# Down projection of two column groups by seven block products instead of plain tiles, in a two-layer hybrid kernel on one core

## What is computed

```python
def swiglu(x, w_gate, w_up, w_down):
    return (jax.nn.silu(x @ w_gate) * (x @ w_up)) @ w_down
...
for l in range(DEPTH):
    x = x + 0.5 * swiglu(rms_norm(x, ffn1_norm[l]), ffn1_w_gate[l], ffn1_w_up[l], ffn1_w_down[l])
    x = x + hybrid_mixer(...)
    x = x + 0.5 * swiglu(rms_norm(x, ffn2_norm[l]), ffn2_w_gate[l], ffn2_w_up[l], ffn2_w_down[l])
```

## Time and profile before

| | |
|---|---|
| median of 3 runs | 2651.4 us (2651.0 to 2652.24) |
| the profiled execution: own time, span | 2651.94 us, 2650.2 us |
| mean granted TensorE clock | 0.999 |
| TensorE matmul busy | 2616.0 us, 99% of the span, 15716 instructions |
| VectorE, ScalarE, GpSimd busy | 1464.2, 1262.9, 1169.5 us (55, 48, 44%) |
| DMA | 240 MB, mean 91 GB/s |

### The profile page before, as it was taken

How to read it: one execution, slowest core, us unless ns; L and a number is a source line. 1 busy time by engine, 2 the same in 40 slices (tenths; PEclk the granted TensorE clock), 3 DMA queues, 4 the chain that set the end, 5 groups by cost and what they waited for, 6 DMA issues and landing times. The chain is left out here.

```text
span 2650.2 us, 41444 instructions
## 1 busy us (share of the span) xinstructions
PE 2616.0 (99%) x15716; PEld 2216.3 (84%) x15716; DVE 1464.2 (55%) x2231; ACT 1262.9 (48%) x2323; POOL 1169.5 (44%) x684
## 2 busy tenths in 40 slices
PE   7999999999999999999999999999999999999999
PEld 6999988766777788898988989887667778898998
DVE  7453574666556368263683535745665653773543
ACT  6453543655534336363464635345555344363543
POOL 4565644211322346565565655432122324465554
PEclk9999999999999999999999999999999999999999
DMA  4322223310111232232223232333012112232322
GB/s 148 112 96 98 103 103 105 110 49 30 71 60 60 84 111 101 96 112 96 96 96 108 100 112 84 107 108 107 33 41 72 61 60 91 104 105 96 112 96 96
DMA packets 38550, 240.46 MB, mean 91 GB/s; under 512 B 4321, under 2 KB 5601, under 8 KB 16353
## 3 DMA queue, kind: packets, MB, share of 16 engines
q1 hardware_dynamic: 36416, 233.85, 25.7%
q10 hardware_dynamic: 1952, 4.12, 0.4%
HBM read 234.81 MB, written 2.10 MB: 89 GB/s over the span
## 5 line engine op out<-in xcount | busy, mean ns | idle before, releaser
L351 POOL TENSOR_TENSOR wlo<-raw,whi 128x1024 fp32r<-128x1024 f32 (+1 forms) x310 | 687.1, 2217 | 1233.9 <-ACT whi L426 803.1
L1633 PE MATMUL bank<-hhi,whi 128*128 128x512 f32 x816 | 339.3, 416 | 15.5 <-DVE hlo L925 10.5
L1739 PE MATMUL bank<-th,slot_u 128*128 128x256 f32 x1152 | 326.3, 283 | 2.1 <-ACT tmp L549 2.1
L426 ACT ACTIVATE whi<-raw 128x1024 fp32r<-128x1024 f32 (+1 forms) x198 | 192.6, 974 | 283.8 <-PE bank L1635 158.1
L1740 PE MATMUL bank<-tl,slot_u 128*128 128x256 f32 x1152 | 326.0, 283 | 0.0
L1635 PE MATMUL bank<-hhi,wlo 128*128 128x512 f32 x816 | 321.0, 393 | 0.0
L1634 PE MATMUL bank<-hlo,whi 128*128 128x512 f32 x816 | 320.2, 392 | 0.0
L1633 PE MATMUL bank<-ff,whi 128*128 128x512 f32 x704 | 274.0, 389 | 0.0
L1634 PE MATMUL bank<-ff,whi 128*128 128x512 f32 x704 | 274.0, 389 | 0.0
L1635 PE MATMUL bank<-ff,wlo 128*128 128x512 f32 x704 | 273.9, 389 | 0.0
L416 ACT ACTIVATE whi<-raw 128x1024 fp32r<-128x1024 f32 (+1 forms) x96 | 96.7, 1008 | 370.4 <-PE bank L1635 370.4
(11 more groups left out here) (348 smaller groups left out, 6266.9 us busy)
## 6 DMA issues: line engine op xcount, KB each, us to landing
raw<-cb SPq DMA_DIRECT2D x48, 768.0 KB, 4.1
raw<-gu0a SPq DMA_DIRECT2D x16, 1024.0 KB, 5.0
raw<-gu0b SPq DMA_DIRECT2D x16, 1024.0 KB, 4.9
raw<-pM SPq DMA_DIRECT2D x16, 1024.0 KB, 4.9
raw<-cq SPq DMA_DIRECT2D x16, 1024.0 KB, 4.9
raw<-gu1a SPq DMA_DIRECT2D x16, 1024.0 KB, 4.8
raw<-gu1b SPq DMA_DIRECT2D x16, 1024.0 KB, 4.9
raw<-gu0c SPq DMA_DIRECT2D x12, 1024.0 KB, 4.9
```

The source lines that it names most:

```text
L351: pool.tensor_tensor(wlo[:, s, 0:w], raw[:, j, lo:lo + w], whi[:, s, 0:w].bitcast(f32), ALU.subtract).then_inc(sem["lo_done"], 1)
L426: A(whi[:, s, 0:(wa, wb)[s]], raw[:, u % 2, s * wa:s * wa + (wa, wb)[s]], ACT.Copy).then_inc(sem["hi_done"], 1)
L1633: mm(outp, wh, mhi, start=start and k == 0, stop=False)
L1739: mm(outp, wh, parts[k][0], start=start and k == 0, stop=False, skip_group_check=True)
```

## The change

The down projection of groups a and b is made by seven block products as well; group c stays plain. For this the hidden tiles of a group take the part of the data: the tile in the first half of the group (c < `KH` = 4) and the one four later are the rows of the 2 x 2 blocks, and token halves are the columns. A down unit makes two output tiles from 8 hidden tiles in 84 matmuls of 256 tokens. The sums of quarters that `th` holds for x have now to be made for the hidden tiles themselves, and for every group again: T3 = B22 - B12, and T2, T1, T4 from it, with highs and lows. They are made tile by tile, as each tile of the second half of a group comes out (`tile_parts`, `sum_highs`, `sum_lows`, and `tile_lows` on POOL). The plain tile of the first half is kept in fp32 (`uf`) beside its high and low. The first down unit after a gate-up unit ("turn") has another order of the products, since the sums of the last tile are still being made: A12, s4, A11, s3, s2, A22, s1, with s4 in a bank half of its own. Weight rows of the down projection are rotated by four tiles on the host.

```diff
-ORDER = ["A11", "A12", "s2", "s3", "s1", "A22", "s4"]
-SPLIT_AT = {0: 1, 1: 2, 4: 3, 3: 4, 2: 5, 5: 6, 6: 7}
...
+BLOCKS = {"reg": ["A11", "A12", "s2", "s3", "s1", "A22", "s4"], "turn": ["A12", "s4", "A11", "s3", "s2", "A22", "s1"]}
+BLOCKS["head"] = BLOCKS["reg"]
+HIGHS = {"head": (0, 1, 5, 4, 3, 2, 6), "reg": (0, 1, 4, 3, 2, 5, 6), "turn": (0, 1, 2, 3, 4, 5, 6)}
...
ScalarE
+                def tile_high(f, U):
...
+                    act.wait_ge(sem["st_p"], me.at("st_p", U.n + 1))
...
+                    elif U.c < KH:
+                        A(k2h[U.p][U.c], r[:], ACT.Copy).then_inc(sem["uhi_ready"], 1)
+                        A(uf[U.c], r[:], ACT.Copy).then_inc(sem["uf_ready"], 1)
+                    else:
+                        A(k1h[U.c - KH], r[:, 0:ST], ACT.Copy).then_inc(sem["uhi_ready"], 1)
+
+                def sum_highs(U):
...
+                    act.wait_ge(sem["u_sum"], me.at("u_sum", 4 * U.q + 1))
+                    A(thu[:, k, T3], tfu[:, k, T3], ACT.Copy).then_inc(sem["u_hi"], 1)
+                    act.wait_ge(sem["u_sum"], me.at("u_sum", 4 * U.q + 4))
+                    A(thu[:, k, T2], r[:, 0:ST], ACT.Copy).then_inc(sem["u_hi"], 1)
+                    A(thu[:, k, T1], r[:, ST:S], ACT.Copy).then_inc(sem["u_hi"], 1)
+                    A(thu[:, k, T4], tfu[:, k, T4], ACT.Copy).then_inc(sem["u_hi"], 1)
...
+                        if tile_before:
+                            late_silu(V)
+                        if U.kind == "turn":
+                            tile_high(f, V)
+                            sum_highs(V)
+                            block_high(6, U)
+                            act.sem_inc(sem["hi_done"], 2)
+                            block_copy(N)
+                            block_high(0, N)
+                            block_high(1, N)
+                            block_snap(p1s[j], bx[j], U, "A11")
+                            block_snap(p7s[j], bw[j], U, "s3")
+                            block_snap(u2s[j], bx[j], U, "s2")
...
VectorE
+                def tile_parts(U):
...
+                        dve.tensor_tensor(k1l[k], r[:, 0:ST], k1h[k].bitcast(f32), ALU.subtract).then_inc(sem["ulo_ready"], 1)
+                        dve.tensor_tensor(tfu[:, k, T3], tfu[:, k, T2], r[:, ST:S], ALU.subtract).then_inc(sem["u_sum"], 1)
...
+                        dve.scalar_tensor_tensor(r[:, 0:ST], tfu[:, k, T3], -1.0, r[:, 0:ST], ALU.mult, ALU.subtract).then_inc(sem["u_sum"], 1)
+                        dve.wait_ge(sem["u_sum"], me.at("u_sum", 4 * U.q + 2))
+                        dve.scalar_tensor_tensor(r[:, ST:S], r[:, 0:ST], -1.0, tfu[:, k, T2], ALU.mult, ALU.subtract).then_inc(sem["u_sum"], 1)
+                        dve.scalar_tensor_tensor(tfu[:, k, T4], r[:, 0:ST], -1.0, tfu[:, k, T4], ALU.mult, ALU.subtract).then_inc(sem["u_sum"], 1)
...
+                def sum_lows(U):
...
+                    dve.wait_ge(sem["u_hi"], me.at("u_hi", 4 * U.q + 3))
+                    dve.tensor_tensor(tlu[:, k, T2], r[:, 0:ST], thu[:, k, T2].bitcast(f32), ALU.subtract).then_inc(sem["u_low"], 1)
+                    dve.tensor_tensor(tlu[:, k, T1], r[:, ST:S], thu[:, k, T1].bitcast(f32), ALU.subtract).then_inc(sem["st_free"], 1)
...
+                        if U.kind == "turn":
+                            tile_parts(V)
+                            sum_lows(V)
+                            block_low(6, U)
+                            first_out(f, U)
+                            block_sums(N)
...
TensorE, the turn
+                        pe.wait_ge(sem["st_free"], me.at("st_free", n - 1))
...
+                        product(0)
...
+                        pe.wait_ge(sem["st_low"], me.at("st_low", 2 * n + 1))
+                        pe.wait_ge(sem["st_snap"], me.at("st_snap", 3 * n + 1))
+                        pe.wait_ge(sem["u_low"], me.at("u_low", V.q + 1))
+                        product(4)
```

More of the change, by code:

```diff
@@ L84, in widths, with block_units, split_at @@
     return WIDTHS.get(name, WIDTHS.get(name[:2], (KD * P, KD * P)))
[L87 to L95, removed]
+def block_units(f):
+    out, g, q = [], (KF - PLAIN) * f, 2 * KH * f
+    for p, (part, _, n) in enumerate(PASSES):
+        for c in range(0 if p else PLAIN, n):
+            u = FIRST[f"gu{f}{part}"] + c
+            out.append(Unit(u, NST * f + len(out), len(out), p, c, False, "reg" if out else "head", g, q))
+            g, q = g + 1, q + (p < 2 and c >= KH)
+        for c in range(KH if p < 2 else 0):
+            u = FIRST[f"dn{f}{part}"] + c
+            out.append(Unit(u, NST * f + len(out), len(out), p, c, True, "reg" if c else "turn", g, q))
+    return out
+def split_at(i, U):
+    return 7 * U.n + HIGHS[U.kind].index(i) + 1
 def build(nc, t, out):
@@ new lines, in _, with block_low @@
+                        unit(1, 0)
+                        unit(1, 1)
+                        units = block_units(f)
+                        def block_low(U, i):
+                            name = BLOCKS[U.kind][i]
+                            at = {"A11": 0, "A12": BLOCK, "A22": 3 * BLOCK}
+                            src = raw[:, U.u % 2, at[name]:at[name] + BLOCK] if name in at else s3[:] if name == "s3" else s4[:]
+                            pool.wait_ge(sem["st_hi"], me.at("st_hi", split_at(i, U)))
+                            return pool.tensor_tensor(bl[i], src, bh[i].bitcast(f32), ALU.subtract)
@@ L907, in _ @@
                 norm(2)
-                for p in range(len(PASSES)):
-                    ffn_pass(1, p)
+                ffn_blocks(1)
         @block.vector
@@ new lines, in ffn_blocks @@
+                def ffn_blocks(f):
+                    units = block_units(f)
+                    for U in units:
+                        V = units[U.i - 1] if U.i else None
+                        N = units[U.i + 1] if U.i + 1 < len(units) else None
+                        if V is None:
+                            plain_product(f, PLAIN - 1)
+                        elif V.down:
+                            down_close(f, V)
+                        else:
+                            block_product(V)
+                        if U.kind == "turn":
+                            tile_parts(V)
[3 more added lines that the diff above has]
+                            block_sums(N)
+                            block_low(4, N)
+                            third_out(f, U)
+                            block_low(2, N)
+                            fourth_out(U)
+                            continue
+                        first_out(f, U)
+                        if V is None:
+                            plain_low(f, PLAIN_ORDER[2])
+                            token_low(f, 3)
+                            plain_low(f, PLAIN_ORDER[3])
+                        elif not V.down:
+                            tile_parts(V)
+                        if V is not None and N:
+                            block_sums(N)
+                        fourth_out(U)
+                        if V is None:
+                            block_sums(N)
+                        if N and N.kind == "reg":
+                            block_low(4, N)
+                        third_out(f, U)
+                        if N:
+                            block_low(2 if N.kind == "reg" else 4, N)
+                        if V is not None and not V.down and V.p < 2 and V.c >= KH:
+                            sum_lows(V)
+                        if N is None:
+                            block_product(U)
+                            tile_parts(U)
+                    dve.wait_ge(sem["st_p"], me.at("st_p", NST * (f + 1)))
+                    dve.wait_ge(sem["st_free"], me.at("st_free", NST * (f + 1)))
```

492 lines of the change are left out of this document (282 added, 210 removed).

## The result

The changed kernel takes **2670.99 us** (median, 2669.49 to 2672.1) where the kernel before takes 2651.82 (2651.0 to 2652.3) on the same chip: a ratio of 1.0074, 95% interval 1.0062 to 1.0086. It is **slower by 19.2 us**, where I had forecast 4.6 less. The profiled execution has 2670.44 us and a span of 2668.6.

A forecast was written before the change was run, and what follows sets the result against it. TensorE's matmul time was taken as the bound, at 99% busy. Against the profiled execution's 2651.94 us, -25.8 + 19.6 + 1.2 + 0.4 = -4.6 gave 2647.3, forecast as 2647 us, range 2640 to 2655.

The forecast's parts named there:

- in one chain, from the end of the last gate-up unit (10.24) on: First down unit: dependent steps from late_silu to A11's snapshot at 18.08, starting product 4 at 18.29 instead of 15.84.
- The turn: First down unit after gate-up: product 4 waits for A11's late snapshot, 2.45 us each, 8 x 2.45 = 19.6 us.
- is not added, since the later chain covers it: Product 0 of the first down unit: its 0.8 us wait for VectorE's lows was left out of the sum.
- The clock: Rival, 3%: TensorE's clock falls at the turns, 2.4 us each, 19 us in all, giving 2666 us.
- the turn's waits are shorter: Argument against a clock fall: matmuls behind a 2.01 us wait ran at full speed, and waits in first down units are shorter.
- The matmuls' saving: Down sections of groups a and b: 40.32 us against 43.55, 3.23 us a section, 25.8 us saved in all.
- Product 6: Gate-up units behind a second-half tile: its bank's release comes up to 0.06 us late, in 20 units, 1.2 us.
- that rival: Rival, 11%: DVE's small instructions delay product 6's bank; at 0.5 us a unit 2656 us, with the turn's excess 2658.
- The first unit: First block unit: token_low(3) on DVE ends late for product 5; TensorE waits 0.1 us each, 0.4 in all.
- cheap turn: Rival, 12%: ACT's snapshot is not last to arrive, only product 0's 0.8 us remains in first down units; 2634 us.
- The rival of closer matmuls: Rival, 2%: matmuls of 256 run closer than 0.12 us (109 ns), some 12 us beyond the forecast, 2635 us.
- the third sign: Sign that the forecast is wrong: matmuls behind a turn take longer than 0.28 us.

The follow-up runs named there:

- the kernel with both moves: Changed kernel with ScalarE's s4 copy behind snapshot 7 in the last gate-up unit and the A11 snapshot earlier in the turn: 2640.12 us, ratio 0.9958 to before.
- the last experiment: The kernel with both moves, plus VectorE's low sums ahead of its combination and GpSimd's T3 low part one place earlier: 2632.66 us, ratio 0.9929 to before.
- two moves worth nothing each: On the kernel with both moves: VectorE's low sums earlier, 2641.37 us; GpSimd's T3 low part earlier, 2640.63 us; together 2632.66 us.
- the kernel before with seven copies: Kernel before plus seven idle ScalarE copies ahead of snapshot 7 in the last gate-up unit of groups a and b: 2681.29 us.
- the kernel with GpSimd's move alone: The kernel with both moves plus GpSimd's T3 low part one place earlier, VectorE's low sums left in place: 2640.63 us.

## Why the prediction was wrong

The four matmul, turn, product-6 and first-unit terms came to -4.6; measured was +19.2. The 24 us between them:

- **Missing altogether, 8 x 2.1 = 16.8 us: the last gate-up unit.** "in one chain, from the end of the last gate-up unit (10.24) on" was the step that failed. Product 5 of that unit waits 2.02 us by the distance of starts, 2.1 with the matmul behind it, and the sum had nothing for it. I took for granted that this unit runs like any other and began to count at its end. But its engines prepare the next unit, and the next unit is the turn, with another order of blocks: the copy that is free in a regular unit waits there for VectorE's last sum. The new order of blocks was in the diff, and my own count had the fourth sum start at 7.41 into such a unit and so end at 8.10, while product 5 wants its bank at 7.20. I used that count for product 6 alone. Moving that one copy recovered 17.1 us (13.6 by waits, 4.0 by the clock).
- **The turn, 3.07 instead of 2.45, 8 x 0.62 = 5.0 us.** The mechanism was right: product 0 waited on VectorE's lows and product 4 on the snapshot, and putting the snapshot earlier recovered 13.9 us, 1.62 in each group without a fall, where product 4's wait was 1.56. That product 0's wait "is not added, since the later chain covers it" was right in kind: what was left at product 4 was the chain's remainder. But the chain started late. `block_product` ran at 106.27, 0.5 us later than behind a silu on time, because VectorE still had the low parts of the tile before to make; those waited for ScalarE's highs, and those stood behind the copy of s4. That this is what made the turn dearer is read from the rows and not shown by a run: with the copy moved behind the snapshots it still waited for the fourth sum, and the chain started no earlier.
- **The clock, 4.0 us, a rival with 3%.** I argued that "the turn's waits are shorter" than a wait of 2.01 us that had no slow matmuls behind it. Product 5's wait was of that very length, 2.02, and the clock fell behind three of the eight, and once more behind a wait of product 4 that had grown to 2.1 us. One such row was too little to exclude a fall. The size I had given, 2.4 us a fall, was too high: 1.55 and less.
- **The matmuls' saving, 3.23 us a section, was right.** A down unit without waits runs at the pitch of a gate-up unit (changed kernel, window of the unit behind the turn, against the second of the earlier trace rows), and in the kernel with both moves a whole down section takes 40.45 us from its first matmul (104.80 to 145.25), where 4 x 10.08 is 40.32:

```profile
118.21:128.29 10.08, 10.08 (x86) 10.08 (x85) 7.98 (x16) 5.92 (x13) 7.44 (x7) 1.00 0.29 105
```

- **Product 6, 20 x 0.06.** In the units behind a second-half tile a wait of 0.06 us showed in the starts, but in 12 of the 20 places: in the last gate-up unit of each group product 5's wait covers it. Its size held, and 0.7 of the 1.2 us is there. DVE decided nothing there, and that rival fell. The first unit waits as before, 0.8 us from start to start.
- The **cheap turn**, 12% at 2634 us, was wrong for this kernel, but its condition was nearly built by the last experiment: -25.8 + 8 x 0.81 + 1.6 = -17.7, and 18.5 was measured.

- **The rival of closer matmuls** was priced wrongly: at 109 ns against the row's 43.55 us a section it would have given 29 us beyond the forecast and not 12. It did not come; they stand 120 ns apart as before.

In the eight groups the parts close: 16.8 + 5.0 + 4.0, less 0.5 for product 6 and 0.4 for the first unit, is 24.9, and from -4.6 to the 20.0 measured there it is 24.6. The 1.6 us gained outside the groups stay unexplained. That these parts add is argued from distances in one trace; what the runs show of them is the 17.1, the 13.9 and their sum.

The signs that were to show the prediction wrong would have missed the step that failed. They looked at the down section and at product 6. The section takes 42.05 us from the turn's first matmul (1080.01 to 1122.06), 43.4 with product 0's wait, both between 41.5 and 43.5; product 6 waits 0.06. Only the third sign came, matmuls longer than 0.28 us, at the turns where the clock fell.

## What to carry to other kernels

Where a unit differs from its neighbours, follow the unit ahead of it too: its engines prepare the special one, and each instruction there that now reads a late operand holds everything queued behind it on its engine, however free it was before. A copy that waits for a sum belongs behind the snapshots whose banks TensorE wants back. And when an edit removes a wait without moving the time, look for a second wait of the same length further on before giving it up: two moves worth nothing each were worth some 8 us together.

## What the hardware showed beyond that

The granted clock near waits of TensorE in the middle of dense work, at the places studied here: behind 74 waits of 0.3 to 1.7 us at and around the turns of the seven kernels with the change it fell at none; of 2.02 us, at 3 of 8 in the changed kernel and 4 of 8 with the snapshot earlier; of 2.05 to 2.42 us (product 4 of the changed kernel, in the turns where the clock had fallen before), at 1 of 3; of 2.76 us, at 7 of 8; of 5.40 us, at 8 of 8, there with each stretch beginning during the wait. At 2.02 us it began from 0.04 to 1.4 us behind the first matmul after the wait, and lasted 3.41 us with matmuls 0.21 apart instead of 0.12. It costs 1.4 to 1.55 us in the kernel before with seven copies; part of that comes back where a later product would have waited anyway (0.6 with the snapshot earlier). A few stretches at half clock lie where no new wait is (at 534 and 1849 us in the kernel before, at 530 for 6.83 us in the kernel with GpSimd's move alone); why, no run here tells.
